# A unit's values behind the first four key granules of the next unit, in a decoder step's sample attention

## What is computed

```python
# A: keys gathered by stride from the window buffer, one softmax for each head group
sc = jnp.einsum('bqhe,bqjhe->bhqj', q, g[:, :, :, 0]) * (e ** -0.5)
p, den, lse = masked_softmax_parts(sc, valid)
o = jnp.einsum('bhqj,bqjhe->bqhe', p, g[:, :, :, 1]) / den[..., None]
# B: 2048 past keys with a bias, and the new keys
s_past = jnp.einsum('bqhe,bkhe->bhqk', q, k_past) * (e ** -0.5) + cq - c_past
s_new = jnp.where(tril, jnp.einsum('bqhe,bkhe->bhqk', q, k_new) * (e ** -0.5) + cq - c_new, -inf)
pr = softmax(concat([s_past, s_new]))
o = einsum(pr[..., :n_past], v_past) + einsum(pr[..., n_past:], v_new)
# both branches, prompt and samples
mix = (sigmoid(ga) * (oa @ w_pa) + sigmoid(gb) * (ob @ w_pb)) @ w_o
```

## Time and profile before

| what | us |
|---|---|
| median of 3 runs | 1154.83 |
| lowest, highest | 1152.92, 1156.64 |
| the profiled execution's own time | 1153.55 |
| its span | 1151.6 |
| sample attention, about | 390 to 748 |

### The profile page before, as it was taken

The page is one execution under the profiler, slowest core; times in us unless marked ns, Lnnn a source line. Parts: engine busy times, 40 slices in busy tenths (PEclk is TensorE's granted clock), DMA queues, the critical chain, the costliest instruction groups (busy, mean ns, idle before and its releaser), DMA issues. The chain is left out here.

```text
span 1151.6 us, 17921 instructions
## 1 busy us (share of the span) xinstructions
PE 995.0 (86%) x7324; PEld 583.3 (51%) x7324; DVE 380.3 (33%) x877; ACT 206.1 (18%) x509; POOL 186.9 (16%) x210
## 2 busy tenths in 40 slices
PE   3999999997899799999899986599959997787760
PEld 2444444444466466666566763264545554454430
DVE  3100033225764456268105740004631230010005
ACT  3000000003454111200210022012311111111114
POOL 0000043302210100122122212000022332222110
PEclk9999999999999799999899998599959999899995
DMA  9997776687769699999699949796279999999956
GB/s 328 357 314 270 259 258 249 234 272 273 234 223 320 199 308 333 345 382 358 243 355 359 352 153 336 312 262 280 95 313 358 370 377 386 381 386 395 412 217 246
DMA packets 96701, 348.47 MB, mean 303 GB/s; under 512 B 11658, under 2 KB 55442, under 8 KB 77294
## 3 DMA queue, kind: packets, MB, share of 16 engines
q1 hardware_dynamic: 79118, 265.89, 64.6%
q0 software_dynamic: 15552, 79.97, 18.7%
q10 hardware_dynamic: 1952, 1.48, 0.5%
HBM read 335.46 MB, written 63.36 MB: 346 GB/s over the span
## 5 line engine op out<-in xcount | busy, mean ns | idle before, releaser
L1615 PE MATMUL bank<-turned,w_all 128*128 128x320 f32 (+1 forms) x512 | 143.0, 423 | 0.0
L459 PE MATMUL bank<-w_all,turned 128*128 128x481 f32 (+2 forms) x384 | 121.0, 507 | 1.1 <-DVE turned L668 1.1
L459 PE MATMUL bank<-w_ring,turned 128*128 128x481 f32 (+2 forms) x384 | 118.4, 502 | 0.0
L2032 PE MATMUL bank<-w_all,mix_row 128*64 128x256 f32 x736 | 95.3, 417 | 24.9 <-DMA w_all<-in_w_exp 23.9
L1615 PEld LDWEIGHTS bank<-turned,w_all 128*128 128x128 f32 x512 | 94.6, 195 | 35.8 <-issue 14.6
L2032 PEld LDWEIGHTS bank<-w_all,mix_row 128*64 128x64 f32 x736 | 62.7, 151 | 64.3 <-issue 43.9
L459 PEld LDWEIGHTS bank<-w_all,turned 128*128 128x128 f32 (+1 forms) x384 | 57.4, 173 | 62.4 <-issue 59.3
L459 PEld LDWEIGHTS bank<-w_ring,turned 128*128 128x128 f32 (+1 forms) x384 | 57.1, 171 | 60.4 <-issue 57.3
L1719 DVE STREAM_TRANSPOSE mods<-w_all 128x2048 f32<-128x2048 f32 (+1 forms) x39 | 86.6, 2239 | 3.4 <-PE bank L1491 2.3
L2078 DVE COPY act_t<-bank 128x128 f32<-128x128 f32 x33 | 9.6, 292 | 199.3 <-PE bank L2042 197.6
L678 DVE COPY w_all<-bank 128x481 f32 (+5 forms) x32 | 16.9, 531 | 152.6 <-PE bank L459 152.4
(11 more groups left out here) (357 smaller groups left out, 1289.1 us busy)
## 6 DMA issues: line engine op xcount, KB each, us to landing
w_all<-in_w_exp SPq DMA_DIRECT2D x22, 2048.0 KB, 39.5
out_a_sample<-in_cache_a SPq DMA_DIRECT2D x8, 4080.0 KB, 21.4
w_all<-in_w_exp SPq DMA_DIRECT2D x25, 1024.0 KB, 37.5
mods<-in_w_ada SPq DMA_DIRECT2D x21, 1024.0 KB, 7.6
w_all<-in_cache_a SPq DMA_DIRECT2D x22, 512.0 KB, 7.1
w_all<-in_cache_a SPq DMA_DIRECT2D x40, 256.0 KB, 6.6
turned<-in_w_exp SPq DMA_DIRECT2D x5, 2048.0 KB, 41.6
mods<-in_w_exp SPq DMA_DIRECT2D x5, 2048.0 KB, 42.9
```

Source lines behind the costliest of these rows:

```text
L459: mm = nc.tensor.matmul(m.banks[i][r:r + ROWS[i], 0:hi - lo], m.hT[:, k, i * P:i * P + ROWS[i]], ring[u][:, CW * k + lo:CW * k + hi], star ...
L1615: mm = nc.tensor.matmul(GATE[:, 0:WIDTH[h]], gate_w[b][k][:, c % 2 * P:(c % 2 + 1) * P], m.hT[:, k, 256 * h:256 * h + WIDTH[h]], start=k = ...
L2032: mm = nc.tensor.matmul(m.banks[2 + p][x * SLOTS:(x + 1) * SLOTS, 0:HID], hgT[:, k, :], m.weights(u)[:, (2 * k + x) * HID:(2 * k + x + 1) ...
```

## The change

`STEPS` is built otherwise. Ahead of the values of units 0, 1 and 2 now stand the first four key granules of the unit that follows (`AHEAD = 4`), and its other keys come behind these values. It is 92 steps still. Unit 1's keys 0 to 3 are steps 7 to 10 and unit 0's values 11 to 17; unit 2's keys 0 to 3 are steps 21 to 24 and unit 1's values 25 to 31; unit 3's keys 0 to 3 are steps 44 to 47 and unit 2's values 48 to 63. From step 64 on (unit 3's keys 4 to 15, its values) and for the 80 merge pieces nothing has another number.

The four granules are two chunks of kind A or one of kind B. Their scores stay in banks 0 and 1 until the first value step, where DVE adds their mask or bias, behind the transposes that have read the old score rows. The fold of a unit moves from behind the second key of the next unit to behind its sixth. Sums of the pages, their DMAs and the bias loads get other steps, relative to unit 0's second value step.

```diff
-    STEPS = [(u, part, g) for u in range(len(UNITS)) for part in "kv" for g in range(COUNT[u])]
+    AHEAD = 4
+    STEPS = [(0, "k", g) for g in range(COUNT[0])]
+    for u in range(len(UNITS)):
+        ahead = AHEAD if u + 1 < len(UNITS) else 0
+        STEPS += [(u + 1, "k", g) for g in range(ahead)]
+        STEPS += [(u, "v", g) for g in range(COUNT[u])]
+        STEPS += [(u + 1, "k", g) for g in range(ahead, COUNT[u + 1] if ahead else 0)]
...
-            if g == 1 and u:
+            if g == AHEAD + 1 and u:
                 use(t, "after", "fold", u - 1, 0)
...
-            if (u, g) == (0, 2):
+            if (u, g) == (0, 1):
                 use(t, "after", "totals", u, 0)
...
+    SUMS = at[(0, "v", 1)]
...
-                        if t == (first + 4 * (x - 1) + 1 if x >= 2 else first - 4):
+                        if t == (at[(u, "k", 4 * (x - 1) + 1)] if x >= 2 else first if u == 2 else first - 4):
                             past_bias(u, x)
-                if t == 13:
+                if t == SUMS + 5:
                     sp.wait_ge(terms, 3)
...
-                if t == 17:
+                if t == SUMS + 8:
                     sp.wait_ge(sorted_c, 4)
...
-                if t == 11:
+                if t == SUMS + 3:
                     act.wait_ge(pre, BH + 4)
...
-                if t == 15:
+                if t == SUMS + 7:
                     act.wait_ge(rows_c_in, 16)
...
-                if t + 1 < N and STEPS[t][1] == "k" and STEPS[t + 1][1] == "v":
+                if t < N and STEPS[t][1] == "k" and STEPS[t][2] + 1 == COUNT[STEPS[t][0]]:
                     exps(STEPS[t][0])
...
-                if c == 0 and u:
-                    dve.wait_ge(p_done, max(n for n, y in enumerate(uses) if y[:2] == ("probs", u - 1)) + 1)
+                if u:
+                    early_use = ("probs", u - 1, 1) if wide(u) * (c + 1) <= AHEAD else ("probs", u - 1, 3 if kind(u - 1) == "a" else 8)
+                    dve.wait_ge(p_done, use_of[early_use] + 1)
...
-                    if part == "k" and ends_chunk(u, g):
+                    if part == "k" and ends_chunk(u, g) and (u == 0 or g >= AHEAD):
                         add_bias(u, chunk_of(u, g))
+                    if part == "v" and g == 0 and u + 1 < len(UNITS):
+                        for c in range(AHEAD // wide(u + 1)):
+                            add_bias(u + 1, c)
...
                     if (u, part, g) == (0, "v", 0):
+                        running_sums()
                         rows_of_pages()
-                    if (u, part, g) == (0, "v", 1):
-                        running_sums()
```

## The result

The changed kernel takes 1155.28 us (median of 22 runs, 1149.65 to 1159.04), the kernel before, beside it, 1151.29 us (22 runs). The ratio is 1.003 (95% interval 1.0016 to 1.0043). The forecast, 0.47% faster, had the wrong sign. Single runs of one kernel here scatter by 4 to 8 us either way. Part of that lies ahead of what was changed: the first key step starts between 386.4 and 395.9 us in the profiled executions. So the experiments are also compared by TensorE's own steps in their traces, counted from this first key step.

What follows compares the result with a forecast made beforehand. TensorE was taken to bound the sample attention, with waits and a slowed clock at unit 2's end. 5.9 - 0.1 + 0.2 - 0.6 = 5.4 us off the 1154.83 median gave 1149.4 us, 0.47% less; range 1146 to 1155.5.

Steps and rivals of the forecast that it cites:

- Unit 2: End of unit 2's keys: 3.22 us of exponential waits and 2.70 us of slow matmuls go, less 0.1 us of tanh wait.
- three candidates for a new wait: Unit 2's end: unit 3's first score behind last adds (no cost), tanh behind exponentials (0.1 us), unit 3's fifth key granule (0 to 0.2).
- Loads, "I count 0": SP and POOL keep five steps' lead, 16.8 us; despite SP's wait for `c_past`, step 27's granule has 4.5 us left; cost 0.
- the loads have no slack: Rival, chance 0.10: DMA queues are full, value granules could come late without the old pause; eats 3 to 4 us, about 1153.
- slower: Rival, chance 0.08: SP's wait for `c_past` delays five value loads and reaches TensorE; 1158 at 13 us more, 1165 at 20.
- The argument against that rival: In the stretch with DMA share 1.00, no TensorE wait for a load stands; 16.8 us of lead against 9.5 us landing.
- Unit 1: Unit 1's end: 1.03 us of waiting goes, 1.5 us for the tanh before piece 22 comes; loss 0.6 us net.
- Units 0 and 1 together: Ends of units 0 and 1: gain 0.2 us at the first, loss 0.6 us at the second.
- `totals`, where I counted 0.3: Unit 0's values: TensorE waits 0.3 us for DVE's later running sums, bounds 0 and 1; net gain there 0.2 us.
- The clock at unit 1's end: Rival, chance 0.12: short idle times make the clock fall at unit 1's end, adding some 2.7 us; 1152.1 us.
- The tail moves as a whole: From step 64 on nothing changes place, so the tail and the phase behind it come about 5 us earlier, otherwise as before.

Runs made afterwards that it cites:

- x_hold: Changed kernel, with GpSimd's gather of unit 2's fifth key granule and all later gathers held until unit 1's last value granule landed; ratio 0.9966, 1148.69 us against 1152.48.
- x_bias_late2: Changed kernel, with SP loading unit 2's first two bias chunks at step 24 instead of 21, run a second time with a new profile; ratio 1.0007.
- x_old_sums_tanh: Changed kernel, with the page sums at their old steps and ACT's exponential of units 0, 1 and 2 behind the following step's tanh; ratio 1.0007.
- x_unit1_only: Kernel before, with only unit 1's first four keys ahead of unit 0's values and the sums moved as in the changed kernel; ratio 1.0013.

## Why the prediction was wrong, step by step

- **Unit 2** (5.9 - 0.1 us): right. 6.3 us in after, 6.2 alone, with the waits for the exponentials gone and the clock at 1.00. Of the three candidates for a new wait only the tanh showed, with 0.24 us.
- **Loads, "I count 0"**: the step that failed. It compared a lead of 16.8 us with landing times read in an order in which value loads of kind A and gathers hardly overlapped, and held them constant in an order in which they do. The lead was not kept either: the late granule's first issue stood 13.4 us ahead of the time at which TensorE was ready for it, and not 16.8. By itself that was harmless, since in x_hold it was 12 us and nobody waited. The place was nearly right: it was argued for SP's wait for `c_past` and the granule of step 27. But that wait was harmless (x_bias_late2, x_old_sums_tanh), and the late granule is that of step 30. It costs 5.8 us of wait, and 0.9 us in the value step behind it (1.94 for 1.07) and 0.5 us in the piece (2.94 for 2.42) at the lower clock, 7.2 us in all. The rival "the loads have no slack" had the symptom and a price of 3 to 4 us; "slower" had it with SP as the mechanism.
- **The argument against that rival** read a full DMA share with no waits as slack. The runs show it was none: some 2 MB less in 98 us, and the gathers beside it, were enough for a wait of 5.8 us.
- **Unit 1** (-0.6 us): the mechanism was right, the size of one term not. The tanh waits behind the exponential as said, but for 3.2 us (3.6, 3.2, 2.5 and 0.9 in other executions with the new sums) and not 1.5. ACT's four sorting activations, 2.20 us, now stand directly in front of the exponential, waiting for the rows of the pages till 469.55; my derivation looked only at DVE in front of it. Counted from the first key step, the exponential began 0.7 us later than forecast, and TensorE was ready for the piece 1.0 us earlier, which makes up the rest. With the old sums the wait is 0.9 to 1.2 us.
- **Units 0 and 1 together**: a loss of 1.3 us, where the sum had 0.4. The waits for the exponentials (0.51 and 1.03 us) and two of 0.17 us for DVE are gone, and the 3.17 us for the tanh are new. TensorE did not wait for DVE at `totals`, where I counted 0.3. With the 7.2 us of the late load, and without unit 1's fold (0.63 us), which is still to come, this is the +7.8 of step 32 to within 0.1.
- **The clock at unit 1's end** (rival, 0.12): it didn't fall behind 3.17 us of idle time there (the piece took 2.39 us). It fell behind 5.82 us at step 30 and behind 3.54 us in x_unit1_only. The rule on short idle times in the Trainium skill (TensorE: Matmul & The Clock Gate, "A second HAM failure mode: psum-queue depth-cycling") has no case in the new falls: each of the two follows one long pause. In before, the fall at unit 2's end came behind two waits of 1.81 and 1.41 us.
- **"The tail moves as a whole"**: nearly. The end of unit 3's keys had a clock of 0.72 in after, 0.86 in before, and 1.3 us were lost there (step 66 at +1.5, step 79 at +2.8). In x_hold the clock was 0.86 and nothing was lost. From step 48 to the output projection the kernels with unit 3's keys ahead differ from before by anything between a gain of 0.9 us and a loss of 2.0. This part is seen, not explained. In after's profile the phase ends 1.9 us longer than in before; the medians are 4.0 us apart, and no trace shows where the rest lies.

## What to carry to other kernels

Moving steps for one engine moves the loads that feed them. Before a load's landing time is taken from a trace, look which other queue was active while it flew; in the new order ask which two queues will be issuing together, and which of the two is due first. If a queue that runs ahead for later work slows the loads that are due now, one wait that holds it back can be cheap, as it was here. And where a change has several parts of one kind, try each alone: here the last of three held the whole gain, and the late load came only with the first.

## What the runs showed of the hardware

- A 256 KB value load landed 6.3 us after its issue (median, 4.9 to 8.0) in before, with no gather issued yet. Beside POOL's gathers it took 10.3 to 15.1 us (four loads, after) and 7.6 to 18.4 us (eight loads, x_bias_late2). With the gathers held it took 4.3 to 7.9 us.
- The issues themselves got longer beside the gathers: eight took 5.58 us at 482.37 and 11.92 us at 490.78, and 6.2 us for the same two granules with the gathers held. What SP had to issue behind them was late by that. Why an issue gets longer is not shown.
- How late the granule was changed from execution to execution of one kernel: waits of 1.4 and 7.0 us. A profile of one execution shows one of these cases; the timed runs (1.0024 and 1.0007) suggest that the good one was not the common one.
